# Feed-forward ups with all 512 tokens in one pass, written out unit by unit; a weight unit of the second mixer split between two turned blocks; 47 slot waits left out on VectorE

## The chip, the cores and the metric

The kernel runs on one core of one Trainium2 chip. The metric is the device time of one execution in microseconds. The kernel before takes 2045.62 us (median of three runs, 2045.24 to 2046.76).

## The reference, cut to what matters

512 tokens of width 1024 go through two layers. Each layer is a mixer and a channel mixer, both with a norm before and a residual add behind. The channel mixer of layer 0 is the dense one that is changed here; that of layer 1 sends each token to 2 of 8 experts.

```
def hybrid_mixer(xn, ...):
    z = einsum("bsd,de->bse", xn, w_in)          # 1024 -> 2560: ten units of 256 columns
    xa, gb, gc, xr, gr = split(z, ...)
    ya = gb * causal_depthwise_conv(gc * xa, ...)
    yr = rg_lru(causal_depthwise_conv(xr, ...), ...) * gelu(gr)
    return einsum("bse,ed->bsd", group_rms_norm(concat(ya, yr)), w_out)

def swiglu(x, w1, w3, w2):                        # dense, 1024 -> 3072 -> 1024
    h = silu(x @ w1) * (x @ w3)
    return h @ w2

for layer in range(2):
    h = h + hybrid_mixer(rms_norm(h), ...)
    h = h + (swiglu if layer == 0 else moe_swiglu)(rms_norm(h), ...)
return rms_norm(h, final_g)
```

## The kernel before, in words

**Two-part products.** Every float32 operand of a matmul is held as two float32r tiles, a rounded one (hi) and the remainder (lo). A product takes three matmuls: hi by hi, hi by lo, lo by hi. Weights arrive by DMA in units of 128 x 2048 float32 (1 MB, in two halves) in `raw`, a ring of 3. ScalarE (ACT) copies each half into `whi` (line 384), VectorE (DVE) subtracts it from `raw` into `wlo` (line 772). `whi` and `wlo` are rings of 6 units. SyncE (SP) issues the loads in order (line 295), each when DVE has done with the same place of the `raw` ring three units earlier.

**The dense feed-forward** (`channel_mixer`, `up`, `down` on PE; `hidden` on ACT and DVE) runs once for each half of the tokens, so all weights are loaded and split twice: 2 x 36 units. A group is three units: 256 columns of w1, 256 of w3, 256 rows of w2. A tile is 128 of the 3072 hidden features, 24 tiles a half. For a tile, `up` does for w1 and for w3, and for each of 8 blocks of the contraction, two matmuls: `whi` as stationary against the hi and the lo tokens side by side (2 x 256 = 512 columns), and `wlo` against the hi tokens (256 columns). The two halves of the PSUM bank are then added: ACT copies one (lines 547, 552), DVE adds the other (lines 995, 999). DVE multiplies by the silu (line 1003), ACT and DVE split the product into `hid` (lines 556, 1007), and `down` of the tile, 12 matmuls of 512 columns with the hidden tile as stationary and the weights moving, comes one tile later. PE turns four tiles per pass of a hardware loop. Between the matmuls of a tile ACT and DVE split half units of the next group (`ahead`), each behind a wait for the ring's place (`group_gate`).

**The turn to the second mixer.** Before the last `down`, PE turns two normed token blocks by transposes (`x_T`, line 1644), ACT and DVE write them as hi and lo into `XN` (lines 423, 800). `second_norm` does the other two blocks. PE runs units 0 and 1 of the mixer first for tokens 0 to 255, with the two remaining `x_T` between, and then for tokens 256 to 511 (`z_tile`). Unit 2 needs the PSUM bank of unit 0, which DVE's causal convolution has to have read (`z_waits`, `xc_ready`; lines 883 and 887). The mixer's units 0 to 2 are split within the feed-forward's last group; units 3 to 5 are split behind the second norm and ahead of the convolution.

## Time and profile before

| | us |
|---|---|
| median of the runs | 2045.62 |
| the profiled execution's own time | 2044.83 |
| its span in the profile | 2043.0 |
| feed-forward, from its first matmul to the first of the second mixer | 197.15 to 603.72 = 406.57 |
| PE busy (matmuls) | 2002.7, 98% |
| DVE busy | 1539.5, 75% |
| ACT busy | 1203.1, 59% |
| mean granted TensorE clock | 0.996 |

Busy times of matmuls come from modelled ends and overlap; how fast PE works is read from the starts of its instructions. In all views L1612 is the one line on which every float matmul is recorded, so groups are told apart by tiles: `PS<-XN,whi` is a product of the tokens with hi weights, `PS<-whi,hid` a down with hi weights. PEld is the weight load that goes with each matmul. The 40 slices of the page show the granted clock at 9 or above everywhere.

### The profile page before, as it was taken

Reading aid. Unit: us, or ns where it says so; the run is one execution under the profiler, and the core shown is the slowest. Engines: PE = TensorE matmul, PEld = TensorE weight load, DVE = VectorE, ACT = ScalarE, POOL = GpSimd, SP = SyncE. Lnnn points to the kernel's source line nnn. Section 1 sums busy time; section 2 is a strip of 40 time slices with the busy share of each in tenths; the row PEclk is TensorE's granted clock in tenths of the full one; section 3 lists DMA queues with packets and bytes.
Section 4 is the critical chain, followed back from the end, with each engine's and each line's share of the span. In section 5 each row is a group of like instructions: output and inputs, shape, how many; then the busy total and the mean of one; then the engine's idle time right before and its main releaser. Section 6 shows DMA issues by size and latency. Waiting matters only on the chain.

```text
span 2043.0 us, 33512 instructions
## 1 busy us (share of the span) xinstructions
PE 2002.7 (98%) x11055; PEld 1740.1 (85%) x11056; DVE 1539.5 (75%) x1702; ACT 1203.1 (59%) x1546; POOL 106.5 (5%) x150
## 2 busy tenths in 40 slices
PE   8999999999999998999999999999999999999997
PEld 8778888888888778999899988888999888889996
DVE  6896766666677986766677689898777798987785
ACT  4443655455555424655565578787665687876552
POOL 1000000100000002200100010100000100001000
PEclk9999999999999999999999999999999999999999
DMA  7321766766653313877687699999877799999881
GB/s 218 129 73 43 229 213 202 221 200 188 189 158 124 113 52 102 278 239 239 207 288 248 205 343 389 359 393 358 306 252 254 274 385 358 390 374 356 262 272 63
DMA packets 245704, 487.51 MB, mean 239 GB/s; under 512 B 16884, under 2 KB 86628, under 8 KB 245652
## 3 DMA queue, kind: packets, MB, share of 16 engines
q1 hardware_dynamic: 237812, 462.04, 66.9%
q0 software_dynamic: 7840, 24.80, 3.4%
q8 instruction: 29, 0.48, 0.1%
q14 instruction: 23, 0.19, 0.0%
HBM read 473.21 MB, written 13.58 MB: 238 GB/s over the span
## 4 chain that ended last, share of the span: by engine, by line
PE 91%; DVE 4%; issue 2%; ACT 1%; DMA 1%; POOL 0%; another core or an unknown queue 0%; DVEq 0%; SPq 0%; ACTq 0%; POOLq 0%
PE PS L1612 90%; ACT whi L384 1%; PE PS L1975 1%; DVE wlo L772 1%; DVE OV L887 1%; PE PS L1644 0%; DVE OV L901 0%; DVE OV L806 0%; DMA OV<-in_norm_mix_g 0%; DMA raw<-in_w_in 0%; POOL SM L1423 0%; DVE RES L981 0%; DMA raw<-in_expert_w 0%; DVE RES L1397 0%
## 5 line engine op out<-in xcount | busy, mean ns | idle before, releaser
L772 DVE TENSOR_TENSOR wlo<-raw,whi 128x1024 fp32r<-128x1024 f32 x872 | 1031.9, 1221 | 195.8 <-ACT whi L384 187.2
L384 ACT ACTIVATE whi<-raw 128x1024 fp32r<-128x1024 f32 x872 | 888.9, 1054 | 252.1 <-PE PS L1612 159.2
L1612 PE MATMUL PS<-XN,whi 128*128 128x512 f32 (+3 forms) x3328 | 951.5, 363 | 14.2 <-issue 3.8
L1612 PE MATMUL PS<-XN,wlo 128*128 128x152 f32 (+3 forms) x2944 | 774.7, 263 | 0.0
L1612 PEld LDWEIGHTS PS<-XN,whi 128*128 128x128 f32 x3328 | 617.7, 188 | 77.5 <-issue 14.1
L1612 PE MATMUL PS<-whi,XN 128*128 128x512 f32 x2208 | 653.6, 394 | 3.8 <-issue 2.2
L1612 PEld LDWEIGHTS PS<-XN,wlo 128*128 128x128 f32 x2944 | 560.9, 191 | 14.4 <-issue 1.6
L1612 PEld LDWEIGHTS PS<-whi,XN 128*128 128x128 f32 x2208 | 411.9, 188 | 95.4 <-issue 6.4
L1612 PE MATMUL PS<-wlo,XN 128*128 128x512 f32 x1216 | 414.7, 391 | 0.0
L1612 PEld LDWEIGHTS PS<-wlo,XN 128*128 128x128 f32 x1216 | 228.4, 188 | 49.3
L1612 PE MATMUL PS<-whi,hid 128*128 128x512 f32 x448 | 130.6, 392 | 0.9 <-DVE hid L1007 0.9
L596 ACT ACTIVATE OV<-PS 128x352 f32<-128x352 f32 x112 | 51.4, 460 | 105.4 <-PE PS L1612 101.8
L1612 PEld LDWEIGHTS PS<-whi,hid 128*128 128x128 f32 x448 | 80.6, 188 | 18.0 <-issue 0.9
L547 ACT ACTIVATE OV<-PS 128x256 f32<-128x256 f32 x48 | 18.4, 383 | 126.6 <-PE PS L1612 126.5
L1048 DVE TENSOR_TENSOR OV<-PS,OV 128x352 f32<-128x352 f32 x112 | 58.2, 521 | 31.3 <-ACT OV L596 26.8
L995 DVE TENSOR_TENSOR OV<-PS,OV 128x256 f32<-128x256 f32 x48 | 20.4, 424 | 80.8 <-ACT OV L547 80.8
L1612 PE MATMUL PS<-wlo,hid 128*128 128x512 f32 x224 | 70.6, 390 | 0.0
L1551 POOL DMA_DIRECT2D y_rows<-OV x14 | 8.1, 577 | 923.5 <-DVE OV L1145 492.5
L913 DVE RECIPROCAL PS<-PS 128x1024 f32<-128x1024 f32 x8 | 52.5, 6560 | 0.6 <-ACT PS L494 0.6
L1612 PEld LDWEIGHTS PS<-wlo,hid 128*128 128x128 f32 x224 | 42.1, 188 | 9.3
L552 ACT ACTIVATE OV<-PS 128x256 f32<-128x256 f32 x48 | 18.4, 383 | 53.4 <-PE PS L1612 53.4
L999 DVE TENSOR_TENSOR OV<-PS,OV 128x256 f32<-128x256 f32 x48 | 20.4, 425 | 29.3 <-ACT OV L552 29.3
(247 smaller groups left out, 967.0 us busy)
## 6 DMA issues: line engine op xcount, KB each, us to landing
raw<-in_expert_w SPq DMA_DIRECT2D x672, 512.0 KB
raw<-in_ffn_w SPq DMA_DIRECT2D x144, 512.0 KB
raw<-in_w_in SPq DMA_DIRECT2D x40, 512.0 KB
raw<-in_w_out SPq DMA_DIRECT2D x16, 512.0 KB
y_rows<-OV POOLq DMA_DIRECT2D x13, 512.0 KB, 6.2
y_rows<-OV POOLq DMA_DIRECT2D x13, 192.0 KB, 7.3
RES<-in_x SPq DMA_DIRECT2D x4, 512.0 KB, 5.7
x_tok<-OV POOLq DMA_DIRECT2D x4, 512.0 KB, 2.9
```

Of the source, the lines that this page charges most:

```text
L384: act.activation(whi[:, u0 % CONV, half(h)], raw[:, r, half(h)], ACT.Copy).then_inc(s["hi_done"], 1)
L547: act.activation(c1[:, b, 0:n], PS[:, b, n:2 * n], ACT.Copy).then_inc(s["c1_done"], 1)
L552: act.activation(c3[:, b, 0:n], PS[:, 2 + b, n:2 * n], ACT.Copy).then_inc(s["c3_done"], 1)
L596: act.activation(low[:, pair(p), :], PS[:, pair(p), WIN:2 * WIN], ACT.Copy).then_inc(s[("w1_low", "w3_low")[part]], 1)
L772: dve.tensor_tensor(wlo[:, w, half(h)], raw[:, u0 % RAW, half(h)], whi[:, w, half(h)].bitcast(F32), ALU.subtract).then_inc(s["lo_done"], 1)
L887: ins = dve.scalar_tensor_tensor(dst[:, back:T], src[:, 0:T - back], prm[:, c:c + 1], dst[:, back:T], ALU.mult, ALU.add)
L913: step(dve.reciprocal(v, v))
L995: dve.tensor_tensor(s1[:, b, 0:n], PS[:, b, 0:n], c1[:, b, 0:n], ALU.add).then_inc(s["s1_done"], 1)
L999: dve.tensor_tensor(hm[:, b, 0:n], PS[:, 2 + b, 0:n], c3[:, b, 0:n], ALU.add).then_inc(s["s3_done"], 1)
L1048: dve.tensor_tensor((up1, hv)[part][:, pair(p), :], PS[:, pair(p), 0:WIN], low[:, pair(p), :], ALU.add).then_inc(s[("w1_sum", "w3_sum")[pa ...
L1612: return pe.matmul(out_, lhsT, rhs, start=start, stop=stop, skip_group_check=True)
L1975: ins = pe.transpose(PS[:, bk, t * P:(t + 1) * P], hM[:, t * P:(t + 1) * P], ident[:, :])
```

## The change

1. The feed-forward takes all 512 tokens at a time and goes twice over half of the 3072 features (`p`). In each pass all ups come first, then all downs: 12 up units (w1 and w3 in turn), then 6 w2 units for tokens 0 to 255 and the same 6 again for tokens 256 to 511. That is 48 units in place of 72. Hi and lo products of an up now go to the same bank: three matmuls of 512 columns per block of the contraction. Only in the first group are they halved (256 columns), since the last token block is turned there. The copies and adds of bank halves are gone, and silu and the product read PSUM.
2. The split hidden tiles (12 of 128 x 512) live in three of the six places of `whi` and `wlo`, so the feed-forward's weights have a ring of 3 there (`slot`, `HID_SLOTS`). Ups and downs change between PSUM banks 0 to 3 and 4 to 7.
3. No hardware loops are left in this stage on any engine.
4. DVE no longer waits for a ring place before a split of the feed-forward; it waits for ACT's hi half only, and ACT waits for the place (47 waits fewer).
5. The second mixer's unit 2 is split between the third and fourth turned block, and on DVE unit 5 comes behind the convolution.

The diff, cut (removed bodies are above; the banks, the zeroing counts and `x_T` are shown where they change):

```
--- before.py
+++ after.py
@@ -41,6 +41,7 @@
+HID_SLOTS = (5, 0, 1)
...
@@ -52,15 +53,15 @@
-F0 = 2
-MIX1_BASE = FFN_BASE + 2 * 3 * FFN_G
+FT = 12
+FPH = 4 * FT
+MIX1_BASE = FFN_BASE + FPH
-MOE_F = F0 + 2 * 2 * FFN_G
+assert FPH % CONV == 0 and FFN_BASE % CONV == 2
...
@@ -237,13 +237,36 @@
             if i >= CONV:
                 eng.wait_ge(s["z_done"], 10 * l + i - CONV + 1)
             elif l > 0:
-                for n in ("w1_done", "w3_done", "w2_done"):
-                    eng.wait_ge(s[n], MOE_F)
-
-        def group_gate(eng, part, f, df):
-
-
-            eng.wait_ge(s[("w1_done", "w3_done", "w2_done")[part]], df + (f - 2))
+                ffn_free(eng, FPH - 3 + i if i < 3 else FPH - 1)
+        def ffn_unit(v):
+            p, r = v // (2 * FT), v % (2 * FT)
+            return p, r // FT, r % FT
+        def ffn_free(eng, v):
+            p, down, n = ffn_unit(v)
+            if down:
+                eng.wait_ge(s["w2_done"], FT * p + n + 1)
+            else:
+                eng.wait_ge(s[("w1_done", "w3_done")[n % 2]], FT * p + n - n % 2 + 2)
+        def slot(u):
+            return 2 + (u - FFN_BASE) % 3 if FFN_BASE <= u < MIX1_BASE else u % CONV
+        def hid_tile(w, j, c0, c1):
+            return w[:, HID_SLOTS[j // 4], 512 * (j % 4) + c0:512 * (j % 4) + c1]
+        def up_bank(p, part, t):
+            return 4 * p + 2 * part + t
+        def down_bank(p, h):
+            return 4 if p == h else 0
...
@@ -311,11 +334,16 @@
-            def group(u0, du, g, a1, a3, a2):
...
+            def feed_forward():
+                for v in range(FPH):
+                    p, down, n = ffn_unit(v)
+                    if down:
+                        k = FT * p + 2 * (n % (FT // 2))
+                        load(FFN_BASE + v, 0, w2_v[:, k:k + 2, :], 2)
+                    else:
+                        c = FT * P * p + 256 * (n // 2)
+                        load(FFN_BASE + v, 0, (w1_v, w3_v)[n % 2][:, :, c:c + 256], KD)
...
@@ -442,6 +465,7 @@
                     act.wait_ge(s["y_evac"], b + 1)
                     squares(2 * TB + b, junk[:, b % 2, :])
                 x_hi(2 * TB + 2)
+                mix_split(1, 2)
                 x_hi(2 * TB + 3)
 
             def norm(q, ready):
@@ -533,28 +557,45 @@
-            def hidden(u0, du, q, f0, df, n):
...
+            def ffn_split(v):
+                ffn_free(act, v - 3)
+                split(FFN_BASE + v, 0, 0)
+            def ffn_silu(p, g, t):
+                n = FT * p + 2 * g + t
+                act.wait_ge(s["w1_done"], n + 1)
+                if n >= 2:
+                    act.wait_ge(s["hm_done"], n - 1)
+                act.activation(sl[:, t, :], PS[:, up_bank(p, 0, t), :], ACT.Silu).then_inc(s["sl_done"], 1)
+            def ffn_hi(p, g, t):
+                act.wait_ge(s["hm_done"], FT * p + 2 * g + t + 1)
+                act.activation(hid_tile(whi, 2 * g + t, 0, T), hm[:, t, :], ACT.Copy).then_inc(s["hh_done"], 1)
+            def feed_forward():
+                for p in range(2):
+                    v0 = 2 * FT * p
+                    for g in range(FT // 2):
+                        ffn_silu(p, g, 0)
+                        ffn_silu(p, g, 1)
+                        ffn_split(v0 + 2 * g + 3)
+                        ffn_hi(p, g, 0)
+                        ffn_hi(p, g, 1)
+                        ffn_split(v0 + 2 * g + 4)
+                    for n in range(FT):
+                        if p == 0:
+                            ffn_split(v0 + FT + n + 3)
+                        elif n < FT - 1:
+                            ffn_split(v0 + FT + n + 3)
+                            if n == FT // 2:
+                                act.wait_ge(s["zero_out"], 1)
+                                for b in range(2):
+                                    act.wait_ge(s["y_evac"], b + 1)
+                                    squares(2 * TB + b, xa[:, b, :])
...
@@ -766,7 +797,7 @@
 
             def split(u0, du, halves=(0, 1)):
 
-                w = u0 % CONV
+                w = slot(u0)
                 for h in halves:
                     dve.wait_ge(s["hi_done"], du * 2 + (2 * u0 + h + 1))
                     dve.tensor_tensor(wlo[:, w, half(h)], raw[:, u0 % RAW, half(h)], whi[:, w, half(h)].bitcast(F32),
@@ -829,6 +860,7 @@
                     mean(2 * TB + b)
                     scaled(2 * TB + b)
                 x_lo(2 * TB + 2)
+                mix_split(1, 2)
                 x_lo(2 * TB + 3)
 
             def last_block():
@@ -938,6 +970,8 @@
                         dve.wait_ge(s["rw_hi"], 1)
                         dve.tensor_tensor(RW[:, :, E:2 * E], praw, RW[:, :, 0:E].bitcast(F32),
                                           ALU.subtract).then_inc(s["rw_ok"], 1)
+                    if l and jj == 0:
+                        mix_split(1, CONV - 1)
                     mix_split(l, 6 + 5 * jj)
                     if jj:
                         pair_norm(l, 1)
@@ -983,30 +1017,63 @@
-            def hidden(u0, du, f0, df, n):
...
+            def ffn_split(v):
+                split(FFN_BASE + v, 0)
+            def ffn_gated(p, g, t):
+                n = FT * p + 2 * g + t
+                dve.wait_ge(s["w3_done"], n + 1)
+                dve.wait_ge(s["sl_done"], n + 1)
+                if n >= 2:
+                    dve.wait_ge(s["hh_done"], n - 1)
+                    dve.wait_ge(s["hl_done"], n - 1)
+                dve.tensor_tensor(hm[:, t, :], PS[:, up_bank(p, 1, t), :], sl[:, t, :],
+                                  ALU.mult).then_inc(s["hm_done"], 1)
+            def ffn_lo(p, g, t):
+                j = 2 * g + t
+                dve.wait_ge(s["hh_done"], FT * p + j + 1)
+                dve.tensor_tensor(hid_tile(wlo, j, 0, T), hm[:, t, :], hid_tile(whi, j, 0, T).bitcast(F32),
+                                  ALU.subtract).then_inc(s["hl_done"], 1)
+            def ffn_add(p, h):
+                dve.wait_ge(s["w2_done"], FT * p + (h + 1) * (FT // 2))
+                for c in range(2):
+                    r = RES[:, 2 * h + c, :].rearrange("p (a n) -> p a n", a=2)
+                    k = down_bank(p, h) + 2 * c
+                    dve.tensor_tensor(r, r, PS[:, k:k + 2, :], ALU.add).then_inc(s["y_evac" if p else "f_add"], 1)
+            def feed_forward():
+                for p in range(2):
+                    v0 = 2 * FT * p
+                    for g in range(FT // 2):
+                        if p and g == 0:
+                            ffn_add(0, 1)
+                        ffn_split(v0 + 2 * g + 3)
+                        ffn_gated(p, g, 0)
+                        ffn_lo(p, g, 0)
+                        ffn_gated(p, g, 1)
+                        ffn_lo(p, g, 1)
+                        ffn_split(v0 + 2 * g + 4)
+                    for n in range(FT):
+                        if n == FT // 2:
+                            ffn_add(p, 0)
+                        if p == 0 or n < FT - 1:
+                            ffn_split(v0 + FT + n + 3)
+                        if p and n == FT // 2:
+                            mean(2 * TB)
+                            mean(2 * TB + 1)
+                            dve.wait_ge(s["gB_in"], 32)
+                            scaled(2 * TB)
+                            scaled(2 * TB + 1)
+                x_lo(2 * TB)
+                x_lo(2 * TB + 1)
+                ffn_add(1, 1)
...
@@ -1234,7 +1301,7 @@
                     constants()
                 else:
                     second_norm()
-                    for i in range(3, CONV):
+                    for i in range(3, CONV - 1):
                         mix_split(1, i)
                 mixer(l)
                 nxt = (FFN_BASE, MOE_BASE)[l]
...
@@ -1486,7 +1536,7 @@
-                pool.wait_ge(s["w1_done"], F0 + 4 * (j + 1))
+                pool.wait_ge(s["w1_done"], 2 * (j + 1))
@@ -1619,10 +1667,7 @@
             def x_T(q, b):
 
                 n = q * TB + b
-                if q == 2 and b < 2:
-                    pe.wait_ge(s["s1_done"], MOE_F)
-                    pe.wait_ge(s["s3_done"], MOE_F)
-                elif q == 2:
+                if q == 2:
                     pe.wait_ge(s["y_evac"], b + 1)
                 elif b >= 2:
                     pe.wait_ge(s["xlo_done"], n - 1)
@@ -1803,62 +1848,69 @@
...
+            def ffn_up(p, g, part, t, n0=0, n1=T):
+                v = 2 * FT * p + 2 * g + part
+                n = FT * p + 2 * g + t
+                u = FFN_BASE + v
+                w = slot(u)
+                bk = up_bank(p, part, t)
+                if n0 == 0 and g:
+                    pe.wait_ge(s[("sl_done", "hm_done")[part]], n - 1)
+                for k in range(KD):
+                    if t == 0 and n0 == 0 and k % 4 == 0:
+                        pe.wait_ge(s["lo_done"], 2 * u + 1 + k // 4)
+                    a = slice(k * 256 + t * P, k * 256 + t * P + P)
+                    mm(PS[:, bk, n0:n1], whi[:, w, a], XN[:, 0, k, n0:n1], k == 0, False)
+                    mm(PS[:, bk, n0:n1], whi[:, w, a], XN[:, 1, k, n0:n1], False, False)
+                    ins = mm(PS[:, bk, n0:n1], wlo[:, w, a], XN[:, 0, k, n0:n1], False, k == KD - 1)
+                if n1 == T:
+                    ins.then_inc(s[("w1_done", "w3_done")[part]], 1)
+            def ffn_down(p, h, q):
+                u = FFN_BASE + 2 * FT * p + FT + (FT // 2) * h + q
+                w = slot(u)
+                for t in range(2):
+                    j = 2 * q + t
+                    pe.wait_ge(s["lo_done"], 2 * u + 1 + t)
+                    if h == 0:
+                        pe.wait_ge(s["hl_done"], FT * p + j + 1)
+                    for n in range(2):
+                        cols = (2 * h + n) * P, (2 * h + n + 1) * P
+                        for xs, ws in ((whi, whi), (whi, wlo), (wlo, whi)):
+                            for c in range(2):
+                                a = t * D + c * 512
+                                ins = mm(PS[:, down_bank(p, h) + 2 * n + c, :], hid_tile(xs, j, *cols), ws[:, w, a:a + 512],
+                                         j == 0 and xs is whi and ws is whi, j == FT - 1 and xs is wlo)
+            def feed_forward():
+                for p in range(2):
+                    if p == 0:
+                        pe.wait_ge(s["xlo_done"], 6)
+                        pe.wait_ge(s["res_done"], 4)
+                        ffn_up(0, 0, 0, 0, 0, HALF)
+                        ffn_up(0, 0, 0, 1, 0, HALF)
+                        x_T(1, TB - 1)
+                        ffn_up(0, 0, 1, 0, 0, HALF)
+                        ffn_up(0, 0, 1, 1, 0, HALF)
+                        pe.wait_ge(s["xlo_done"], 8)
+                    else:
+                        pe.wait_ge(s["f_add"], 2)
+                    for g in range(FT // 2):
+                        for part in range(2):
+                            for t in range(2):
+                                ffn_up(p, g, part, t, HALF if p + g == 0 else 0)
+                    for h in range(2):
+                        if p:
+                            pe.wait_ge(s["f_add"], 4)
+                        for q in range(FT // 2):
+                            if p and h and q == FT // 2 - 1:
+                                x_T(2, 0)
+                                x_T(2, 1)
+                            ffn_down(p, h, q)
...
```

How the instructions stand: TensorE in the feed-forward before, at the end of one tile's w3 up and through its neighbour's down (`XN` the tokens, `hid` the hidden tile).

```order
L1612 MATMUL PS<-XN,whi 128x512
L1612 MATMUL PS<-XN,wlo 128x256
L1612 MATMUL PS<-XN,whi 128x512
L1612 MATMUL PS<-XN,wlo 128x256
L1612 MATMUL PS<-whi,hid 128x512 x2
L1612 MATMUL PS<-wlo,hid 128x512 x2
L1612 MATMUL PS<-whi,hid 128x512 x4
L1612 MATMUL PS<-wlo,hid 128x512 x2
L1612 MATMUL PS<-whi,hid 128x512 x2
```

TensorE in the kernel after, at the end of the first pass's ups and the start of its downs (hidden tiles now lie in `whi` and `wlo`, so both operands of a down have those names).

```order
L1660 MATMUL PS<-XN,whi 128x512 x2
L1660 MATMUL PS<-XN,wlo 128x512
L1660 MATMUL PS<-XN,whi 128x512 x2
L1660 MATMUL PS<-XN,wlo 128x512
L1660 MATMUL PS<-whi 128x512 x2
L1660 MATMUL PS<-wlo,whi 128x512 x2
L1660 MATMUL PS<-whi,wlo 128x512 x2
```

A pair of 512 and 256 columns became a triple of 512; the downs kept their 512 columns.

VectorE before, from the feed-forward's last residual adds to the second mixer's convolution (L1261 the adds, L806 the scaled tokens, L800 `XN` lo, L772 weight splits, L883 and L887 the convolution).

```order
L1261 TENSOR_TENSOR RES<-RES,PS 128x1024 x2
L781 TENSOR_SCALAR SM<-SM 128x1
L806 SCALAR_TENSOR_TENSOR OV<-RES,SM,OV 128x1024
L781 TENSOR_SCALAR SM<-SM 128x1
L806 SCALAR_TENSOR_TENSOR OV<-RES,SM,OV 128x1024
L800 TENSOR_TENSOR XN<-PS,XN 128x8x128 x2
L772 TENSOR_TENSOR wlo<-raw,whi 128x1024 x6
L883 TENSOR_SCALAR OV<-PS,prm 128x512
```

The same place on VectorE in the kernel after (L1048, L837, L831, L803, L915 are the lines now).

```order
L1048 TENSOR_TENSOR RES<-RES,PS 128x1024 x2
L812 TENSOR_SCALAR SM<-SM 128x1
L837 SCALAR_TENSOR_TENSOR OV<-RES,SM,OV 128x1024
L812 TENSOR_SCALAR SM<-SM 128x1
L837 SCALAR_TENSOR_TENSOR OV<-RES,SM,OV 128x1024
L831 TENSOR_TENSOR XN<-PS,XN 128x8x128
L803 TENSOR_TENSOR wlo<-raw,whi 128x1024 x2
L831 TENSOR_TENSOR XN<-PS,XN 128x8x128
L803 TENSOR_TENSOR wlo<-raw,whi 128x1024 x4
L915 TENSOR_SCALAR OV<-PS,prm 128x512
```

Behind the last `XN` block four half splits stand ahead of the convolution in place of six; two stand ahead of that block, and two moved behind the convolution.

## Rows read from the trace of the kernel before

**Rows 1.** The page's parts 1 and 4: busy times; chain by engine.

```profile
PE 2002.7 (98%) x11055; PEld 1740.1 (85%) x11056; DVE 1539.5 (75%) x1702; ACT 1203.1 (59%) x1546; POOL 106.5 (5%) x150
PE 91%; DVE 4%; issue 2%; ACT 1%; DMA 1%; POOL 0%; another core or an unknown queue 0%; DVEq 0%; SPq 0%; ACTq 0%; POOLq 0%
```

**Rows 2.** Chain in order of time, feed-forward: start us, us, what.

```profile
197.15 5.79 PE PS L1612 x32
...
210.00 184.73 PE PS L1612 x968
...
397.74 201.60 PE PS L1612 x1056
599.34 1.75 PE PS L1644 x16
```

**Rows 3.** Timeline of TensorE, one up and down: start us, us, instruction, count.

```profile
229.91 0.40 PE L1612 MATMUL PS<-XN,whi 128*128 128x512 f32 x1
...
234.86 0.40 PE L1612 MATMUL PS<-XN,whi 128*128 128x512 f32 x1
...
235.21 0.63 PE L1612 MATMUL PS<-whi,hid 128*128 128x512 f32 x2
...
237.96 0.39 PE L1612 MATMUL PS<-XN,whi 128*128 128x512 f32 x1
```

**Rows 4.** Timeline of TensorE in the first mixer, triples of 512 columns.

```profile
84.88 0.63 PE L1612 MATMUL PS<-XN,whi 128*128 128x512 f32 x2
...
95.09 0.62 PE L1612 MATMUL PS<-XN,whi 128*128 128x512 f32 x2
```

**Rows 5.** Timeline of TensorE, start of the second mixer, triples of 256 columns.

```profile
603.72 0.30 PEld L1612 LDWEIGHTS PS<-XN,whi 128*128 128x128 f32 x2 [0.32 <-DVE XN L800]
...
604.06 0.28 PE L1612 MATMUL PS<-XN,wlo 128*128 128x256 f32 x1
...
609.46 0.28 PE L1612 MATMUL PS<-XN,wlo 128*128 128x256 f32 x1
```

**Rows 6.** Chain, expert stage: 72 matmuls of 512 columns.

```profile
1226.12 16.57 PE PS L1612 x72
```

**Rows 7.** Windows: us; PE, PEld, DVE, ACT, POOL busy (count), granted clock, DMA share, GB/s.

```profile
210.00:394.00 184.00, 184.00 (x965) 156.97 (x966) 116.30 (x157) 96.76 (x157) 7.31 (x14) 1.00 0.68 215
630.00:729.00 99.00, 99.00 (x412) 77.00 (x410) 85.37 (x81) 42.43 (x48) 1.14 (x2) 1.00 0.28 96
1226.00:1290.00 64.00, 64.00 (x287) 52.28 (x286) 58.67 (x55) 51.87 (x55) 0.00 (x0) 1.00 1.02 381
```

**Rows 8.** Timeline of TensorE: waits of the feed-forward, in brackets.

```profile
210.00 0.69 PE L1612 MATMUL PS<-whi,hid 128*128 128x512 f32 x2 [0.65 <-DVE hid L1007]
...
397.74 0.73 PE L1612 MATMUL PS<-whi,hid 128*128 128x512 f32 x2 [0.27 <-DVE hid L1007]
```

**Rows 9.** Groups by line, 210 to 394 us: the two split operations.

```profile
L772 DVE TENSOR_TENSOR wlo<-raw,whi 128x1024 fp32r<-128x1024 f32 x68 | 83.2, 1223 | 12.8 <-ACT whi L384 11.5
L384 ACT ACTIVATE whi<-raw 128x1024 fp32r<-128x1024 f32 x67 | 70.3, 1049 | 0.0
```

**Rows 10.** Timeline of VectorE, from the last turned block to the convolution.

```profile
616.59 6.89 DVE L772 TENSOR_TENSOR wlo<-raw,whi 128x1024 fp32r<-128x1024 f32 x6
623.40 0.81 DVE L883 TENSOR_SCALAR OV<-PS,prm 128x512 f32<-128x512 f32 x1
```

**Rows 11.** Timeline of ScalarE there: splits of the seventh unit.

```profile
623.02 1.06 ACT L384 ACTIVATE whi<-raw 128x1024 fp32r<-128x1024 f32 x1 [1.92 <-PE PS L1612]
624.54 1.06 ACT L384 ACTIVATE whi<-raw 128x1024 fp32r<-128x1024 f32 x1 [0.47 <-DMA raw<-in_w_in]
```

**Rows 12.** Timeline of TensorE there: before and behind the wait.

```profile
628.46 0.28 PE L1612 MATMUL PS<-XN,wlo 128*128 128x256 f32 x1
629.68 0.74 PE L1612 MATMUL PS<-XN,whi 128*128 128x512 f32 x2 [0.95 <-DVE OV L887]
```

**Rows 13.** Timeline of VectorE behind the convolution: its next idle time.

```profile
638.51 0.69 DVE L898 SCALAR_TENSOR_TENSOR OV<-OV 128x512 f32<-128x512 f32 x1 [4.35 <-ACT OV L475]
```

151 lines of the change are left out of this document (8 added, 143 removed).

## The prediction

> **What bounds the kernel now.** I read the page's busy times and its chain by engine first [rows 1]: the matmul engine is busy 98% of the span and stands for 91% of the chain that ended last. The reader is to see that little work of another engine can be worth anything unless TensorE waits for it. Then the chain in order of time over the stage that changes [rows 2]: from 210.00 us on it is one run of 184.73 us with 968 matmuls, and from 397.74 another of 201.60 us with 1056. A tile of the feed-forward has 32 matmuls in its ups and 12 in its down, so these are 22 and 24 tiles, 8.40 us each, and TensorE has hardly a hole in them. Third, the windows [rows 7]: in the same stretch DVE is busy 116 of 184 us, ACT 97, the DMA engines 68% of the time, all at a granted clock of 1.00, the 2.4 GHz level. So the time of this stage is the number of matmuls times the distance between their starts, and I read that distance in the timeline of TensorE, form by form.
>
> **The ups.** In the kernel before, 14 pairs (512 columns, then 256) run from 229.91 to 234.86: 4.95 / 14 = 0.354 us a pair [rows 3]. From the whole run, (8.397 - 2.75) / 16 = 0.353, where 2.75 is the down from 235.21 to 237.96 [rows 3]. I take 0.353. One block of the contraction of one tile, for 512 tokens, costs two pairs, 0.706. After the change it is a triple of 512 columns. The first mixer runs this very triple: 15 of them from 84.88 to 95.09 give 10.21 / 15 = 0.681 [rows 4]. The number of columns is the same, 1536; the gain of 0.025 comes from one third fewer starts per column for the short form. There are 24 tiles x 2 (w1, w3) x 8 = 384 such blocks. 32 of them (first group, 4 tile parts x 8) are halved, as triples of 256 columns: 15 from 604.06 to 609.46 give 0.360 [rows 5], so 0.720 for all tokens. Sum: 352 x 0.681 + 32 x 0.720 = 239.7 + 23.0 = 262.7 us, against 384 x 0.706 = 271.1. That is -8.4 us.
>
> The bounds of this term. The triple of rows 4 ran beside light transfers, as in the second mixer's window with 28% of DMA time [rows 7]. The expert stage, with the DMA engines full [rows 7], spaces 512 columns by 16.57 / 72 = 0.230 [rows 6]; a triple would be 0.690 and the ups 266.0 us, -5.1. The changed ups ask for one unit of 1 MB per 16 triples, 10.9 us, about 96 GB/s, the same as the second mixer's window, so I take 0.681. On the other side 0.227 is the least distance that I see for this form.
>
> The Trainium skill, "TensorE: Matmul & The Clock Gate", section Back-to-back issue gap, puts the isolated gap at N / 2.4 + 2.5 ns, so 216 ns for 512 columns and 109 for 256, nearly proportional to the columns. By that rule the ups would cost the same before and after within 1 us, which speaks against this change. The rows differ from it: 0.354 for a pair, not 0.325, and 0.681 for a triple, not 0.648.
>
> **The downs.** They have 576 matmuls of 512 columns before and after. Before, 12 take 2.75 us, 0.229 each [rows 3]. Afterwards they demand a unit of 1 MB every 24 matmuls, 5.5 us, some 190 GB/s, against 215 in the window before [rows 7]. I take 0. Bounds: at 0.227 as in rows 4, -1.2; at 0.230 as in rows 6, +0.6.
>
> **Waits of TensorE that go.** Before the first down of the first half and the last down of that half it waits 0.65 and 0.27 us for the hidden tile's lo part [rows 8], since a down follows its own up by one tile. Afterwards all 12 tiles of a pass are turned out by ups, and the down of tile 0 comes 5 groups later. Before the second mixer it waits 0.32 us for the turned block's lo part [rows 5], since only one tile's down, 2.75 us, lies behind the transposes; now a whole unit of 5.5 us lies there. From the end of the last down but one, t, ACT has a weight unit (2 x 1.05, [rows 9]) and DVE its second half by t + 3.3; then DVE writes the two blocks, which have the shape of a weight half, 2 x 1.22, by t + 5.8. TensorE asks at t + 1.75 + 5.5 = t + 7.2. Sum -1.2 us. The three sets of transposes stay (one is the 1.75 us in rows 2).
>
> **The second mixer's start.** TensorE stands 0.95 us before its third unit and is released by DVE's convolution [rows 12]. The convolution begins at 623.40, behind six half splits from 616.59 on, 1.15 us each [rows 10]. It needs unit 0 for all tokens, and ACT, which waits for the same event, is released at 623.02 [rows 11]. Four splits in place of six end at 621.2. What is late next is that event: the convolution can start 0.4 us earlier, not 2.3. The price elsewhere: DVE has two more half splits behind the convolution, 2.3 us, and it was idle for 4.35 us there [rows 13], so they fit. The two moved ahead of the last turned block fall into a hole of DVE, since it waits for TensorE's transpose; ACT's two fit between the transposes in the same way. Through the ring of raw, unit 5's load now starts only when unit 2 is split, some 14 us later than it could; a half took 5.7 us to land there (the split that made room ended at 618.9, the ACT half that waited for DMA began at 624.54 [rows 11]), and ACT has it in time for unit 6, whose slot it gets at 623.02. Term: -0.4 us, bounds 0 and -0.95.
>
> **Edits with no price.** ACT's and DVE's copies and adds of bank halves go: those engines have 87 and 68 us free in the window of 184 [rows 7], and TensorE covers them. The 47 waits on DVE were met whenever ACT's hi half was there; DVE's idle time ahead of its splits is 12.8 us in 68, nearly all for ACT [rows 9], and hidden too: 0. SP issues 96 half loads in place of 144, which relieves DMA, not the bound. TensorE's new waits (banks free, f_add, lo halves) each ask for something done at least one group or six units earlier; behind them stand only its own matmuls. The code of the stage is now straight, as the mixers' is, and theirs shows no hole in rows 4.
>
> **The sum.** -8.4 - 1.2 - 0.4 = -10.0 us. The profiled execution took 2044.83 with a span of 2043.0: it would be 2034.8 with a span of 2033.0. It lies 0.8 below the median of the runs, so for the median 2045.6 - 10.0 = 2035.6 us. The feed-forward would last 406.6 - 9.6 = 397.0 us.
>
> **Rivals.**
> A. *The ups run at the distance of busy stages.* For: before, the pair runs beside 215 GB/s and all forms under load are some ns longer [rows 6, 7]. Against: the ups now need under half of that traffic. -5.1 - 1.2 - 0.4 with the downs at +0.6 gives -6.1: 2039.5.
> B. *Only columns count.* If the long form under the feed-forward's own reads cost two thirds of a pair's time per 512 columns, the triple would be 0.706 and nothing would be won but the waits, and the halved group lost 0.4: -1.2: 2044.4, no change. For: the columns are equal in number, 589,824. Against: rows 3, 4 and 5, where columns alone do not give the times. The Trainium skill's gap rule named above would end here too.
> C. *The ring of three starves the downs: slower.* In a down phase a slot is freed every 5.5 us; then ACT takes 2 x 1.05 and DVE 1.22 more [rows 9], 3.3 us, and 11 us of matmuls are in hand. The load of the unit after that is issued only when that split is done, and must land within 3 x 5.5 - 3.3 = 13.2 us. From there on it binds: at a landing of 16 us a unit costs (16 + 3.3) / 3 = 6.4 us, and 24 down units lose 22 us: 2045.6 - 10.0 + 22 = 2057.6. It turns the whole slower only beyond some 14.5 us. For: lookahead falls from six split units to three, and DVE also has residual adds and scaled tokens to do in the second down phase. Against: 5.7 us to land in the mixer, and before, 1 MB per 5.6 us was kept up without a hole.
> D. *The waits don't go but move*, to the turns between passes, where hi, lo, add and split meet on DVE: up to 1 us at each of four turns, 2039.6. Against: two units are in hand at each.
>
> **How the numbers follow.** Forecast 0.75 (own range 2033 to 2038). A and D together 0.14, B 0.05, C 0.05, the rest 0.01 for something unseen on the fast side. Low end: the downs at 0.227 and all of the 0.95, -11.8, and 1 us of spread: 2033. High end: A with 1.5 us: 2041. That leaves out B and C and tails of the others, some 1.5 in 10. What differs by less than 0.2%, 4.1 us, can't be told from no change. Faster by more than that: forecast, A, D, with part of their tails lost, 0.89. Same: 0.06. Slower: 0.05.
>
> **What the changed profile would show.** Triples of the ups 0.681 apart (0.690 for A, 0.706 for B); the first mixer matmul behind the feed-forward near 594 us, without a wait; downs 2.7 to 2.75 per 12; no wait of TensorE for weights in the two down phases (C: waits for DVE wlo or DMA raw at each unit, growing from the third); the wait before the second mixer's third unit near 0.6 us. The forecast would be wrong if TensorE shows holes of over 0.3 us at unit borders, or if the stages behind the second mixer, which are untouched, changed their length.

## The result

The kernel after takes 2030.95 us (median of four runs, 2029.33 to 2032.64) against 2045.99 for the kernel before beside it: ratio 0.9929, 95% interval [0.9917, 0.9941]. It is faster by 15.0 us, where 10.0 were forecast, and 2030.95 lies below the predicted range. In the profiled executions the gain is 12.2 us of span; the stages, in us (before, after, difference; the last parts are cut where TensorE turns the next expert's tokens):

| stage | before | after | | forecast |
|---|---|---|---|---|
| to the feed-forward | 197.15 | 195.97 | -1.18 | 0 |
| feed-forward | 406.57 | 395.68 | **-10.89** | -9.6 |
| second mixer to its third unit | 25.96 | 25.48 | -0.48 | -0.4 |
| from there to the expert stage | 174.24 | 174.24 | 0.00 | 0 |
| first, second expert visit | 183.50, 182.57 | 183.07, 184.31 | +1.31 | 0 |
| other experts ("third and fourth visit", three experts each), tail | 873.01 | 872.05 | -0.96 | 0 |

The first row is scatter: the same kernel profiled again starts at 197.46. The feed-forward is not: it lasts 395.67 or 395.68 in all fourteen profiles of the kernel after and of its variants that keep its ups.

The page of the kernel after, parts 1 and 4, against [rows 1]:

```profile
PE 1994.3 (98%) x10767; PEld 1728.0 (85%) x10768; DVE 1442.5 (71%) x1514; ACT 1118.7 (55%) x1354; POOL 110.2 (5%) x150
PE 91%; DVE 4%; issue 2%; DMA 1%; ACT 1%; POOL 0%; DVEq 0%; SPq 0%; ACTq 0%; POOLq 0%
```

DVE lost 97 us of work and ACT 84, and neither shows in the time; TensorE stayed at 98%. Its chain in the feed-forward, against [rows 2]:

```profile
195.97 5.98 PE PS L1660 x48
201.96 0.87 PE PS L1689 x8
202.83 381.78 PE PS L1660 x1752
584.61 1.75 PE PS L1689 x16
586.35 11.21 PE PS L1660 x72
```

One piece of 1752 matmuls without a hole: the two waits of [rows 8] and the 0.32 of [rows 5] are gone, and none for weights came. Timeline of TensorE in the ups (against [rows 3, 4]) and in the first down phase, and two windows of ups and downs (columns as in [rows 7]):

```profile
240.36 0.62 PE L1660 MATMUL PS<-XN,whi 128*128 128x512 f32 x2
...
250.56 0.62 PE L1660 MATMUL PS<-XN,whi 128*128 128x512 f32 x2
```

```profile
333.75 0.62 PE L1660 MATMUL PS<-whi,wlo 128*128 128x512 f32 x2
...
340.55 0.62 PE L1660 MATMUL PS<-whi,wlo 128*128 128x512 f32 x2
```

```profile
221.00:327.00 106.00, 106.00 (x470) 87.78 (x469) 36.77 (x39) 31.21 (x40) 9.60 (x17) 1.00 0.44 138
331.00:394.00 63.00, 63.00 (x279) 52.19 (x278) 30.64 (x27) 23.35 (x24) 0.00 (x0) 1.00 0.61 191
```

15 triples in 10.20 us: 0.680 each. 30 down matmuls in 6.80 us: 0.2267 each, at 191 GB/s as reckoned. The ups ran beside 138 GB/s, where 96 were reckoned, and kept 0.680. So up to 191 GB/s load doesn't lengthen a matmul of 512 columns, and in a long run of them it has one pace in ups and downs.

The starts of TensorE's matmuls split the whole stage. After the change its parts begin at 195.97, 202.59 and 394.04 (ups), 328.76, 524.60 and 586.11 (downs):

```profile
328.76 0.62 PE L1660 MATMUL PS<-whi 128*128 128x512 f32 x2
...
524.60 0.62 PE L1660 MATMUL PS<-whi 128*128 128x512 f32 x2
```

| us, from start to start | before | after | |
|---|---|---|---|
| ups, without the wait of 0.65 | 270.9 | 262.6 | -8.3 |
| downs, without the waits of 0.27 and 0.32 | 132.0 | 130.7 | -1.35 |
| transposes | 2.46 | 2.46 | 0 |
| the three waits | 1.24 | 0 | -1.24 |

### The profile page after: what moved, and what is told of

Read it like the earlier page. It is cut to its first block, busy times and chain, and to the rows that moved or that the text cites. A ratio compares the mean times of both kernels' runs of the same rounds, so it can differ in the third digit from the quotient of the medians.

```text
span 2030.8 us, 31497 instructions
## 1 busy us (share of the span) xinstructions
PE 1994.3 (98%) x10767; PEld 1728.0 (85%) x10768; DVE 1442.5 (71%) x1514; ACT 1118.7 (55%) x1354; POOL 110.2 (5%) x150
## 4 chain that ended last, share of the span: by engine, by line
PE 91%; DVE 4%; issue 2%; DMA 1%; ACT 1%; POOL 0%; DVEq 0%; SPq 0%; ACTq 0%; POOLq 0%
PE PS L1660 90%; DVE wlo L803 1%; DMA raw<-in_expert_w 1%; PE PS L2027 1%; DVE OV L919 1%; PE PS L1689 0%; ACT whi L407 0%; DVE OV L933 0%; DVE OV L837 0%; DMA OV<-in_norm_mix_g 0%; POOL SM L1473 0%; DMA raw<-in_w_in 0%; DVE RES L1015 0%; DVE RES L1447 0%; DVE OV L915 0%
## 5 line engine op out<-in xcount | busy, mean ns | idle before, releaser
L803 DVE TENSOR_TENSOR wlo<-raw,whi 128x1024 fp32r<-128x1024 f32 x824 | 970.2, 1221 | 327.4 <-ACT whi L407 323.2
L407 ACT ACTIVATE whi<-raw 128x1024 fp32r<-128x1024 f32 x824 | 834.8, 1054 | 328.7 <-PE PS L1660 231.9
L1660 PE MATMUL PS<-XN,whi 128*128 128x512 f32 (+3 forms) x3392 | 921.3, 358 | 11.3 <-DVE wlo L803 3.2
L1660 PE MATMUL PS<-XN,wlo 128*128 128x152 f32 (+3 forms) x2592 | 715.5, 276 | 0.0
L1660 PEld LDWEIGHTS PS<-XN,wlo 128*128 128x128 f32 x2592 | 496.0, 191 | 24.8
L1660 PE MATMUL PS<-whi 128*128 128x512 f32 x192 | 59.2, 389 | 0.0
L1660 PE MATMUL PS<-whi,wlo 128*128 128x512 f32 x192 | 59.1, 389 | 0.0
L1660 PE MATMUL PS<-wlo,whi 128*128 128x512 f32 x192 | 59.1, 389 | 0.0
L1660 PEld LDWEIGHTS PS<-wlo,whi 128*128 128x128 f32 x192 | 36.0, 188 | 7.5
L1660 PEld LDWEIGHTS PS<-whi,wlo 128*128 128x128 f32 x192 | 36.0, 188 | 7.5
```

The source lines that it names most:

```text
L407: act.activation(whi[:, slot(u0), half(h)], raw[:, r, half(h)], ACT.Copy).then_inc(s["hi_done"], 1)
L803: dve.tensor_tensor(wlo[:, w, half(h)], raw[:, u0 % RAW, half(h)], whi[:, w, half(h)].bitcast(F32), ALU.subtract).then_inc(s["lo_done"], 1)
L1660: return pe.matmul(out_, lhsT, rhs, start=start, stop=stop, skip_group_check=True)
```

## Experiments

### The feed-forward: code, form, or what stands ahead

**e1, e2.** The kernel before with TensorE's loop over tiles written out (e1), with ACT's and DVE's too (e2).

```
-                with pe.Fori(0, loops) as it:
+                for it in range(loops):
```

> The kernel before, with TensorE's loop over four tiles of the feed-forward written out (five turns in each half); nothing else differs. Theory A, forms: in the trace of before the pair of 512 and 256 columns was 353 ns because of its short form, and only the turns of the loop go, 10 x 0.08 us: about 2045, 0 to 1 us faster, pairs still 353 ns and downs 229 ns apart. Theory B, code: inside the loop every matmul comes late by some ns (before the loop the pair was 230 + 116 = 346 ns, in it 236 + 117 = 353; the expert stage's loop spaces 512 columns by 230 where straight code has 226.6). Then straight code has pairs at 346 and downs at 226.6: 768 x 0.007 + 576 x 0.0025 = 6.8 us less, about 2039.

> The kernel before, with the feed-forward's loops written out on TensorE, ScalarE and VectorE (SyncE's load loop stays). Theory A: as the run with TensorE alone, 0 to 1 us faster than before. Theory B: as that run too, about 2039, since only TensorE's own code sets the distance of its matmuls; if ScalarE's and VectorE's loops had a part in the waits of 0.65 and 0.27 us, up to 1 us less than that run.

2048.45 us, ratio 1.0019 [1.0009, 1.0028], and 2048.75, 1.0020 [1.0010, 1.0029]. Pairs and downs keep their distances and the feed-forward its length (406.72 and 406.74 us, before 406.57). Theory B falls: straight code gives nothing here. It even costs 4 us, and not in this stage: the first expert visit lasts 188.0 and 186.3 us, before's 183.5.

**e4.** The kernel after with each triple written as the pair of before (the sum of the bank halves is left out, so tokens go to other experts and the total can't be compared; the feed-forward alone is read).

```
-mm(PS[:, bk, n0:n1], whi[:, w, a], XN[:, 0, k, n0:n1], ...)      (and lo by whi, hi by wlo)
+for c in (0, HALF):
+    mm(PS[:, bk, 0:T], whi[:, w, a], XN[:, :, k, c:c + HALF], ...)
+    ins = mm(PS[:, bk, 0:HALF], wlo[:, w, a], XN[:, 0, k, c:c + HALF], ...)
```

> The kernel after, but its ups of whole tiles in the old form: for each block of the contraction and each half of the tokens one matmul of 512 columns (hi and lo tokens side by side) and one of 256, both into the tile's bank. It leaves out the sum of the two halves of a bank and so computes another function; the copies and adds are not put back, so that TensorE's form alone is timed. Theory A: pairs at 353 ns, 0.706 against 0.681 per block, 352 blocks: +8.8 us. Theory B: straight code has pairs at 346 ns, 0.692: +3.9 us. If only columns count: +0.

The feed-forward is 9.4 us longer, 405.05 against 395.68, and the pair's distance is 0.353 in straight code. The downs, of which 24 to 288 stand in a row here, run at 0.2267:

```profile
344.85 0.62 PE L1660 MATMUL PS<-whi,wlo 128*128 128x512 f32 x2
...
350.29 0.62 PE L1660 MATMUL PS<-whi,wlo 128*128 128x512 f32 x2
```

24 in 5.44 us. That a block costs 26 ns less as a triple has two parts of about 13 ns. Four starts become three: 256 columns in a row are 120 ns apart, so two of them are 240, where one of 512 is 227. And a 512 and a 256 in turn are 353 ns, not 227 + 120 = 347, twice a block. (Only before's first 16 pairs, behind a wait, ran at 230 + 116 = 346.)

In the kernel before, the down of [rows 3], from 235.21 to 237.96, has between those rows

```profile
236.14 1.07 PE L1612 MATMUL PS<-whi,hid 128*128 128x512 f32 x4
237.05 0.62 PE L1612 MATMUL PS<-wlo,hid 128*128 128x512 f32 x2
```

The four matmuls from 235.21 to 236.14 are 0.2325 apart, the next eight 0.2275. Over 44 of the 48 downs (the others stand behind a wait, behind transposes or behind another down), the first five are 232 ns apart on average (228 to 236) and the last seven 226.8: 26.5 ns per down and 1.27 us over 48. The downs pay for something ahead of them.

**e15.** The kernel before with the 512-column matmul over hi and lo tokens written as two of 256 (its accumulation is then started twice in a bank, which changes the values; the feed-forward alone is read).

```
-  mm(PS[:, bk, 0:2 * n], whi[:, w, a], XN[:, :, k, xo:xo + n], k == 0, False)
+  mm(PS[:, bk, 0:n], whi[:, w, a], XN[:, 0, k, xo:xo + n], k == 0, False)
+  mm(PS[:, bk, n:2 * n], whi[:, w, a], XN[:, 1, k, xo:xo + n], k == 0, False)
```

> The kernel before with each feed-forward up's matmul over two blocks of 256 columns written as two matmuls of 256: three of one width in place of a wide and a narrow one. By the first pass of the kernel after (triples of 256 columns at 0.120 a matmul) a pair's 0.353 becomes 0.360, 768 times, 5.4 us more. Theory 'narrow matmuls leave the slow pace behind' (anything of 256 columns ahead of a down slows its first five matmuls): the downs stay at 2.74 per 12, feed-forward 407.0 + 5.4 = 412.4. Rival 'the change of width within the ups does it': downs 2.72 per 12, 411.1.

The feed-forward lasts 411.98 us where before's lasts 406.57: 5.4 longer, as the theory has it, and not the rival's 4.1 (407.0 and 412.4 in the expectation are counted to another mark). "Narrow matmuls leave the slow pace behind" holds against the rival. The timeline of TensorE over one of its downs:

```profile
234.86 0.63 PE L1612 MATMUL PS<-whi,hid 128*128 128x512 f32 x2
...
237.61 0.40 PE L1612 MATMUL PS<-XN,whi 128*128 128x256 f32 x2
```

Again 2.75 us for 12, with ups of a single width ahead. The kernel after has the same once, in its ups, where the first wide triples follow the narrow ones: five matmuls from 219.93 to 221.09, 232 ns each, and the next at 227.

```profile
219.93 0.63 PE L1660 MATMUL PS<-XN,whi 128*128 128x512 f32 x2
...
221.09 0.39 PE L1660 MATMUL PS<-XN,wlo 128*128 128x512 f32 x1
```

But narrow matmuls ahead are not the whole cause. In e4 the first down stands right behind before's pairs, and there only its first matmul is slow, at 235 ns: four take 0.91 us, where before's take 0.93.

```profile
332.94 0.28 PE L1660 MATMUL PS<-XN,wlo 128*128 128x256 f32 x1
333.06 0.62 PE L1660 MATMUL PS<-whi 128*128 128x512 f32 x2
...
333.97 0.62 PE L1660 MATMUL PS<-whi,wlo 128*128 128x512 f32 x2
```

That is 9 ns for the run in place of 26.5. The pairs' distances repeat over three pairs (241 + 120, 236 + 113, 233 + 117 ns); e4's down follows the first of the three and before's the second. And before's down at 210.00, behind the wait of 0.65 us, is slow in its first matmul alone. What sets the size stays open.

### The second mixer's start

**e12.** The kernel after with unit 5 split ahead of the convolution on DVE again, both halves.

```
-                    if l and jj == 0:
-                        mix_split(1, CONV - 1)
...
-                    for i in range(3, CONV - 1):
+                    for i in range(3, CONV):
```

> The kernel after with the last column block of the second mixer's third unit split by VectorE ahead of the convolution's first turn again, as before; all else as after. The forecast's step: the convolution comes 0.4 us later, the wait of TensorE's first matmul of the third unit grows from 0.57 to 0.95 to 1.0 us, and the stretch from the first to the third unit's first matmul from 25.48 to 25.9 us. Rival (the turn was never late, and the 0.48 us came from the feed-forward's new order on VectorE): stays 25.5. Feed-forward stays 395.68.

TensorE's wait before the third unit, of after and of e12:

```profile
617.13 0.73 PE L1660 MATMUL PS<-XN,whi 128*128 128x512 f32 x2 [0.57 <-DVE OV L919]
```

```profile
618.84 0.73 PE L1658 MATMUL PS<-XN,whi 128*128 128x512 f32 x2 [0.95 <-DVE OV L919]
```

And the convolution's first instruction on DVE there:

```profile
610.84 0.81 DVE L915 TENSOR_SCALAR OV<-PS,prm 128x512 f32<-128x512 f32 x1 [1.81 <-PE PS L1660]
```

```profile
612.55 0.81 DVE L915 TENSOR_SCALAR OV<-PS,prm 128x512 f32<-128x512 f32 x1
```

The stretch is 25.86 in e12 and 25.48 in after: 0.38 us, the term. The feed-forward is 395.67 (e12 was run once, 2033.59 us in all). In after DVE stands 1.81 us for TensorE, the event that is late next, as forecast.

### The 47 waits, and code on VectorE

**e16, e18.** The kernel after with `ffn_free(dve, v - 3)` put back ahead of the split in `ffn_split`, twice; **e17** with the same wait written four or six times, 128 instructions in all in place of 47.

```
+                ffn_free(dve, v - 3)                                   (e16, e18)
+                for _ in range(6 if v % 4 and v != 10 else 4):         (e17)
+                    ffn_free(dve, v - 3)
```

> The kernel after with the 47 waits of VectorE for a free weight slot put back ahead of the feed-forward's splits. The forecast costed their absence at nothing: feed-forward 395.68 as without them. Rival (the waits held VectorE up once TensorE's reads became faster, and so its weights): a wait of TensorE for wlo in the downs and a feed-forward above 396.0.

> The kernel of e16_after_waits_back once more, with more runs. Theory 'place of VectorE's code': every run near 2065 to 2070, VectorE without an instruction for 10 to 12 us at each change of expert visit and 30 or more 8192-byte instruction transfers between 1158 and 2037 us, where after has 7. Rival (a disturbance of that one run): 2031.

> The waits for a free slot put back ahead of each of the 47 splits and repeated until they add 128 instructions to VectorE's program (e16_after_waits_back has 47 more than after): VectorE waits for the slots as in e16, and its expert loops stand where after's stand within blocks of 128 instructions (64 bytes each, the 8192-byte transfers on the instruction queue). Theory 'place of VectorE's code': the 10-us stretches without an instruction are gone, third and fourth visit 421 each, median 2029 to 2034 as after. Rival 'the waits themselves': 440 and 435 again, 2067.

e16, run once: feed-forward 395.68, but 2069.28 us in all. e18: 2070.87 (2065.14 to 2071.71), ratio 1.0112 [1.0088, 1.0137]. e17: 2030.88, ratio 0.9927 [0.9908, 0.9946], with 395.67 and 421.4 and 420.9 in the third and fourth visit, where e16 has 444.6 and 435.1. What VectorE waits for in e16 (us in total, times, longest), and its timeline at one of the five places of the third and fourth visit where it stands 9.9 to 12.5 us (the sixth stall, 8.1 us, is in the second visit, and e18 hasn't it):

```profile
DVE wlo L803 <- issue: 49.5, 4, 12.5
DVE OV L1116 <- issue: 17.9, 2, 9.9
```

```profile
1184.53 2.36 DVE L803 TENSOR_TENSOR wlo<-raw,whi 128x1024 fp32r<-128x1024 f32 x2 [12.21 <-issue]
```

The page's part 3, transfers of instructions and their MB, of e16 and of e17:

```profile
q14 instruction: 53, 0.43, 0.1%
```

```profile
q14 instruction: 24, 0.20, 0.0%
```

With the same waits and the loops moved on by 81 instructions more, to after's place within 128, the stalls and 29 of the transfers are gone. The waits cost nothing; the place of the code costs 38 us (by the ratios of e18 and e17). A transfer is 8.2 kB here. The change took instructions of DVE out, these 47 among them, and happened to leave its loops at a good place: after's third and fourth visit last 842.4 us together, before's 843.4.

### The expert visits: code on TensorE, and the clock

e3 is the kernel after once more. e5 and e6 were to move TensorE's code by idle instructions, but `pe.nop()` leaves none in the program: both are the kernel after again.

> The kernel after once more, to part its gain from the scatter of its runs (2029.3 to 2032.6 in four). If the granted clock behind the router's stage explains the scatter, a run with a mean clock of 0.996 or 0.997 lies near 2029.5 and one with 0.994 near 2032.3. Feed-forward 395.7 us long again in either case.

> The kernel after with 64 idle instructions put on TensorE into a branch at the head of the experts' loop that is not taken in the first visits. They are not executed there, but everything behind them on TensorE lies 64 instructions further on. Theory P, pages: TensorE's instructions arrive in transfers of 16384 bytes (queue 8), and in before and in the kernel before written out TensorE stood 1.75 and 3.9 us in the first expert's loop, just while such a transfer ran, at another matmul in each; in the kernel after it didn't stand there. Then a shift alone, with no work changed, brings or moves such a hole of 1 to 4 us in the first visits. Theory Q: the holes came from transfers of weights or from the clock: no hole linked to a transfer of queue 8, times as the kernel after within its scatter.

> The same with 128 idle instructions, half a transfer of 16384 bytes. Theory P: a hole of 1 to 4 us in the first visits at another place than with 64 or with none, or none at all if the jumps again fall well; first expert visit 180 to 188 us long by that. Theory Q: as the kernel after.

2033.44 (e3), 2028.48 (e5) and 2032.88 us (e6, on e5's chip and in its minutes); ratios 0.9947 [0.9934, 0.9960], 0.9918 [0.9905, 0.9932], 0.9941 [0.9927, 0.9954]. One program, medians 4.4 us apart: the scatter is beyond the intervals of single comparisons. The mean clock orders the runs only roughly: e3's at 0.995 are 2031.37 to 2033.44. As nothing was moved in e5 and e6, they say nothing on theory P or Q.

**e9, e10, e11.** 32, 50 (in the kernel after) or 40 matmuls (in the kernel before) in a branch that is never entered. Each counts as two instructions.

```
                 with pe.If(c > 2):
-                    pe.nop()
+                    keep_busy(32, 4)      (e10: 50; e11, in before: 40)
```

> The kernel after with 32 more matmuls (64 instructions of TensorE, a weight load and a matmul each) in the branch of the experts' loop that these inputs never enter. Nothing more is executed, but every later branch of TensorE's program lies 64 instructions further: the branch that the first expert visit jumps to has 53 instructions left to the end of its block of 256, where after has 117, before 48 and the kernels with the written-out feed-forward loop 24. Theory 'fetch' (a taken jump close ahead of a block's end lets TensorE run out of instructions): a hole of 1.5 to 1.8 us in the first visit about 21 us into the expert stage, as before's 1.51 us at 830.7; first visit 182.0 to 182.6 without a long stretch at half clock at its start, 184.5 to 185 with one. Rival 'clock only' (the first visit's length follows the half-speed stretches alone): no such hole, 180.3 to 180.8 or 183.1. Feed-forward 395.68 under both. Whole time 2032 to 2035.

> The same with 50 matmuls (100 instructions) in the branch that is never entered: 17 instructions are left to the end of the block. Theory 'fetch': a hole of 3.9 to 4.2 us at the same place, a little more than the 3.55 us of the kernel with 24 left; first visit 184.2 to 184.9, or 187.0 to 187.5 with the long half-speed stretch; whole time 2034 to 2037. Rival 'clock only': no hole, 180.3 to 183.1, whole time 2031.

> The kernel before with 40 matmuls (80 instructions) in the branch of the experts' loop that is never entered: the branch that the first visit jumps to has 224 instructions left to its block's end instead of 48. Theory 'fetch': before's hole of 1.51 us at 830.7 is gone, and the first visit is shorter by 1.7 us (181.8 at the same clock, where before's profile has 183.5); whole time 1 to 2.5 us under before. Rival 'clock only': the hole stays, no difference.

e11: 2039.67 against 2046.78 beside it, ratio 0.9969 [0.9957, 0.9981]. e10: 2026.55, ratio 0.9907 [0.9888, 0.9926]. e9: 2033.30, 0.9935 [0.9910, 0.9961]. The waits of TensorE from 808 to 1150 us, of before, of e11, of e9, and of e10:

```profile
PE PS L1612 <- issue: 3.3, 2, 1.8
PE PS L1612 <- DVE wlo L772: 3.0, 1, 3.0
```

```profile
PE PS L1612 <- DVE OV L1048: 1.9, 2, 1.8
```

```profile
PE PS L1660 <- issue: 3.1, 2, 2.5
PE PS L1660 <- DVE OV L1115: 1.7, 1, 1.7
```

```profile
PE PS L1660 <- issue: 0.4, 1, 0.4
```

The longer of before's two issue waits, 1.76 us at 818.40, is none of the code's: e11 has it too, 1.75 us, with DVE OV L1048 named, and after has it with 1.73. The two holes meant are these, 27 us into the first visit and 14 us into the second; then the first of them in e1, and the second of them in after, which hasn't the first:

```profile
830.71 0.33 PE L1612 MATMUL PS<-XN,whi 128*128 128x352 f32 x1 [1.51 <-issue]
1001.00 0.42 PE L1612 MATMUL PS<-XN,whi 128*128 128x352 f32 x1 [2.99 <-DVE wlo L772]
```

```profile
832.22 0.25 PE L1612 MATMUL PS<-XN,wlo 128*128 128x176 f32 x1 [3.55 <-issue]
```

```profile
988.18 0.42 PE L1660 MATMUL PS<-XN,whi 128*128 128x352 f32 x1 [3.15 <-DVE wlo L803]
```

Nothing is executed in e11 that before doesn't execute, and both holes are gone: second visit 179.36 us in place of 182.57. (The first is 182.99 against 183.50: its first 80 matmuls took 13.6 us, before's 12.5, at a lower clock.) So the second hole is code too, though the view names DVE for it in before and after: in e3, e9 and e14 the view has no releaser for it:

```profile
984.69 0.42 PE L1660 MATMUL PS<-XN,whi 128*128 128x352 f32 x1 [2.32 <-issue]
```

That the place of the code makes the holes holds against "clock only". That TensorE waits there for a transfer of instructions is argued, not shown: e11 has one transfer more on queue 8 than before (30 and 29), not fewer. My sizes for e9 and e10 were wrong: holes of 0.67 and 0.38 us in the first visit, not 1.5 and 4; and I had not seen the second one, which e9 has (2.48) and e10 has not. Counting instructions to a block's end did not give a hole's size, nor which visit has one.

**e8, e13, e14.** e8: 12 idle matmuls behind `gT_ext(0)`, ahead of the expert stage. e13: these and 38 matmuls in the branch, which puts the loops where e10 has them. e14: the kernel after beside e13.

```
             gT_ext(0)
+            keep_busy(12, 4)
```

> The kernel after with 12 idle matmuls of 128 columns on TensorE behind the transposes of the first gathered block, where it stood 3.1 us in the profile of after. In that profile the granted clock then fell to half for 10.2 us from 787.2 on, in that of before for 3.4 us from 805.2 on. If this drop explains part of the scatter between runs and follows from TensorE's idle stretch, the drop goes or shortens and the median falls by 1 to 2 us with less scatter. If the drop comes from something earlier, it stays, and the time is that of the kernel after.

> The kernel after with 38 matmuls in the branch that is never entered, and 12 idle matmuls between the last transposes ahead of the expert stage and its first matmul: the expert code lies at the places of e10_after_moved_100, the one with both instruction holes gone, and TensorE is kept busy over the wait that a long half-speed stretch followed. Theory (holes and clock are two terms that add up): first visit 179.3 to 179.9, second 179.3, median 2025 to 2028, 3 to 5 us under the kernel after on the same chip. Rival (e10's gain was scatter of the clock): within 1.5 us of the kernel after.

> The kernel after as it is, on the chip and in the minutes of e13_after_moved_busy, to compare them directly. Expected median 2030 to 2033, 13 to 15 us under before; first visit 183.1 with the long half-speed stretch or 180.3 without, second visit 184 with its hole of 3 to 3.5 us.

e8: 2031.3, ratio 0.9939 [0.9925, 0.9952], first visit 180.83. The half-speed stretch ahead of the expert stage is gone, but the median is no lower than those of the kernel after on that chip (2028.48 and 2032.88). e13: 2026.98 (2026.28 to 2027.95), ratio 0.9918 [0.9905, 0.9932]. e14: 2031.83 (2028.59 to 2033.98), ratio 0.9944 [0.9931, 0.9958]. Windows ahead of the expert stage of after and of e13 (the third number from the end is the granted clock):

```profile
786.00:796.00 10.00, 6.80 (x30) 6.41 (x31) 9.01 (x36) 2.26 (x7) 0.00 (x0) 0.56 0.34 107
985.00:995.00 10.00, 6.84 (x39) 6.82 (x39) 3.35 (x3) 3.10 (x3) 1.16 (x2) 0.83 0.94 348
```

```profile
786.00:796.00 10.00, 9.02 (x71) 8.74 (x71) 9.01 (x36) 2.25 (x7) 0.00 (x0) 1.00 0.35 109
985.00:995.00 10.00, 10.00 (x75) 9.82 (x74) 4.60 (x6) 5.57 (x9) 1.61 (x4) 1.00 0.92 332
```

In after's profile the granted clock is at 1.2 GHz for 10.2 us from 787.2 on. That begins within the transposes, ahead of TensorE's wait of 2.71 us (788.66 to 791.37) before its first expert matmul, so this wait is not what it follows; another 3.4 us come at 807.7. The first visit is 183.07. In e3 and e14 the clock falls only when that wait ends, for 3.4 us, and the first visit is 180.31 and 180.46. Behind the second hole the clock falls again (3.4 us from 988.6). In e13 both windows are at 2.4 GHz, and the visits are 180.25 and 180.31 us.

e13 is 4.85 us under the kernel after beside it, and its five runs lie below all five of that one. Its second visit lacks the hole of 2.32 us, which the profiles show. Beyond that the gain is not told from scatter: e5 and e6, one program in the same minutes, were 4.4 us apart. That the idle matmuls add to it is not shown either: e10, without them, came as low on another chip (2026.55), and its visits are shorter, 179.28 and 179.33 us.

**e7.** The kernel after with the experts' loops over groups written out on TensorE.

```
-                with pe.Fori(1, GROUPS) as g:
+                for g in range(1, GROUPS):
```

> The kernel after with TensorE's loop over an expert's seven groups written out, for the narrow and the wide visit; the loop over experts stays. For: a turn of the narrow visit's loop costs 0.2 us beside its transposes, and 6 groups x 5 or so visits turn. Against: TensorE's code for the experts grows about six times, and each visit has to jump over the other kind's code and fetch its own anew. Theory P says the long jumps cost 1 to 4 us at every visit, against some 0.2 x 6 us won: slower by 5 to 20 us. The rival, that jumps cost nothing once TensorE's queue is full: faster by 3 to 8 us.

2108.7 us, ratio 1.0313 [1.0299, 1.0327]. That is 78 us above the kernel after, where 5 to 20 were expected. Its waits of TensorE (after has 3 of this kind in all, 2.7 us) and its transfers of instructions (38 in after):

```profile
PE PS L1660 <- issue: 62.0, 14, 10.6
```

```profile
q8 instruction: 136, 2.23, 0.4%
```

14 stalls of up to 10.6 us, and the clock at 0.979. The Trainium skill, "Runtime: NRT & Kernel Launch", section Instruction fetch mechanics, says that instructions stream in blocks of 16 KiB, 256 instructions, one after the other, and that a taken branch out of what is held must wait for its block. The transfers of q8 fit it (2.23 MB / 136 = 16.4 kB), and so do e7's stalls with 98 transfers more; those of q14 are half as big. The page says too that for this reason kernels prefer full unrolling where possible. The measurements decide against that here: with this loop written out the kernel takes 2109 in place of 2031. The visits still jump past whole branches, which are longer now.

## Why the prediction was wrong

The direction, the place and the main mechanism, the distance between matmuls, were right; the size was not. Two steps failed: the downs were put at 0 and gave -1.35 us, and the stages behind were put at 0 as "untouched", while a hole of TensorE of 1.5 us went from the first expert visit. By its steps:

- **The ups** (-8.4): right, -8.3. 0.680 a triple, not 0.681; rival A's 0.690 and B's 0.706 fall. e4 gives for the 352 blocks 9.4 us where I had 8.8. The narrow triples ran at 0.360, as read. My reason was loose: "one third fewer starts" is four starts that become three, and that is half of the gain; the other half is the turn between widths, which I did not name. The gap rule of the Trainium skill, "TensorE: Matmul & The Clock Gate", section Back-to-back issue gap, which the prediction names, would have, by an estimate from it, a triple at 0.648 and no gain; neither is so.
- **The downs** (0, bounds -1.2 and +0.6): **a failed step.** They gave -1.35, beyond the lower bound. I read 0.229 as the pace of a down under load, and rows 4's 0.227 as the pace without; in fact before's downs were slow in their first five matmuls, behind narrow ones (1.27 us in all), and under 191 GB/s the new ones run at 0.2267.
- **The waits that go** (-1.2): all gone, -1.24. With the ups and downs that is the feed-forward's -10.89. Rivals C and D fall: no wait for weights, none at the turns.
- **The second mixer's start** (-0.4): -0.48, by e12 0.38.
- **Edits with no price**: in themselves right for the 47 waits (e17), but each instruction taken out moves the code behind it. On DVE this could have cost 38 us and did not. The prediction had no term for it.
- **"The stages behind are untouched"** (0): **the other failed step.** They are untouched in work, not in place. TensorE's hole of 1.5 us in before's first visit (e15 has it with 1.39) is missing in all nine profiles with after's TensorE code. The second hole stayed (after 3.15, e14 2.32 us).
- **The sum.** Six medians of the kernel after or of e17, whose TensorE code lies the same, have ratios 0.9929, 0.9947, 0.9918, 0.9941, 0.9944 and 0.9927: mean 0.9934, -13.5 us. The profiles give -10.9 for the feed-forward and -0.5 for the mixer; 1.5 for the first hole brings it to -12.9. The 1.5 us from -13.5 to the -15.0 of the result I take for scatter. It goes with the clock in after's four runs (2032.64 is at 0.994 and 2029.33 at 0.997), but not always: e14 has 2031.83 at 0.997. So of the 5 us between forecast and result, 1.4 are the feed-forward and the mixer, some 1.5 the hole, 1.5 scatter, and 0.6 is not accounted for. That the hole's absence is worth its length in the median is argued from e11, not shown for after by itself: after's own profile has a first visit only 0.43 us shorter than before's, as its clock was at half for 13.6 us in and ahead of it and before's for 6.8.

## What to carry to other kernels

Read the distance between matmuls by their position behind a change of form, not as a mean over the group: a few ns on the first ones can be the neighbour's cost and go with it. Where a kernel has hardware loops with branches, an edit elsewhere can move them and cost or give back more than the edit is worth (here 38 us for 47 waits, some 6 us in e11 for matmuls that never ran). Look at "issue" waits and at the count of instruction transfers before you judge an edit, and try a few places; the count showed the stalls of e16 and e7, but not TensorE's holes of 1 to 3 us. Repeat the kernel beside itself before you explain 0.2%.
